# Sample rows and expert logits through column groups, gate/up weights in quarters, loops written out

## What is computed

```
proj    = rmsnorm(x) @ w_in                      # 53 column tiles of 128
mixers  = rwkv7, pooling, conformer conv, mamba2 SSD   # sequential, 128 rows a turn
merged  = sum_k (branch_k @ w_branch_k) * gate_k
x       = x + merged @ w_out                     # 1032 x 1024 x 1024
h       = rmsnorm(x)
logits  = h @ [w_group | w_expert]               # 4 + 16 = 20 columns
gate    = top-1 group, top-2 experts in it
x       = x + sum_e gate_e * (silu(h @ Wg_e) * (h @ Wu_e)) @ Wd_e   # 16 experts, hidden 256
y       = rmsnorm(x)
```

## Time and profile before

| what | us |
|---|---|
| three runs | 1785.87, 1785.58, 1779.35 (median 1785.58) |
| the profiled execution | 1770.31 |
| its span, first to last instruction | 1768.6 |

### The profile page before, as it was taken

One profiled execution on the slowest core, in us unless ns is written; L12 is line 12 of the kernel. 1 busy time (PEld: TensorE's weight loads), 2 busy tenths in 40 slices (PEclk: granted clock), 3 DMA queues, 4 the chain that ended last, 5 costly groups with the idle time before them and its releaser, 6 DMA issues.

```text
span 1768.6 us, 21208 instructions
## 1 busy us (share of the span) xinstructions
PE 1585.7 (90%) x7922; PEld 997.6 (56%) x7922; DVE 673.8 (38%) x1259; ACT 367.1 (21%) x648; POOL 189.4 (11%) x296
## 2 busy tenths in 40 slices
PE   8999799997799999999999999999999588978950
PEld 5666466564577777777777765666445432322310
DVE  5040079545434345343353432577112401101108
ACT  3110231130232313313133135100012111101102
POOL 3008100030101011010110000000000011101100
PEclk9999899998899999999999999999999689989985
DMA  6111101154111111111111121455201378666636
GB/s 191 36 36 36 28 25 36 36 92 47 59 35 48 45 47 46 39 42 44 48 45 43 38 98 44 153 229 208 81 24 60 119 285 340 241 242 226 218 128 264
DMA packets 38614, 181.38 MB, mean 103 GB/s; under 512 B 5448, under 2 KB 5864, under 8 KB 29440
## 3 DMA queue, kind: packets, MB, share of 16 engines
q1 hardware_dynamic: 22384, 114.03, 18.7%
q0 software_dynamic: 16144, 66.10, 11.4%
HBM read 336.93 MB, written 38.21 MB: 212 GB/s over the span
## 4 chain that ended last, share of the span: by engine, by line
PE 83%; DMA 7%; DVE 5%; issue 2%; ACT 2%; SPq 0%; POOL 0%; DVEq 0%; ACTq 0%; POOLq 0%
PE ps L457 35%; PE ps L810 7%; PE ps L867 7%; PE ps L779 6%; PE ps L881 3%; DMA arena<-in_w_gu 3%; PE ps L724 3%; PE ps L638 2%; PE ps L633 2%; DMA scr<-h_rows,idx 2%; PE ps L616 2%; PE ps L643 2%; PE ps L472 1%; PE ps L798 1%; DVE arena L1657 1%
## 5 line engine op out<-in xcount | busy, mean ns | idle before, releaser
L457 PE MATMUL ps<-arena,wring 128*128 128x344 f32 x2208 | 669.2, 453 | 0.0
L457 PEld LDWEIGHTS ps<-arena,wring 128*128 128x128 f32 x2208 | 406.5, 190 | 192.9 <-issue 5.2
L867 PE MATMUL ps<-arena,scr 128*32 128x512 f32 x1280 | 151.4, 625 | 22.9 <-DMA arena<-in_w_gu 22.9
L1739 POOL DMA_DIRECT2D gate_scratch<-stage x96 | 52.0, 542 | 759.1 <-ACT stage L1020 524.3
L810 PE MATMUL ps<-arena 128*128 128x512 f32 (+1 forms) x288 | 125.6, 594 | 1.2 <-DVE arena L1511 1.2
L779 PE MATMUL ps<-arena,wring 128*128 128x344 f32 x384 | 111.2, 451 | 0.0
L867 PEld LDWEIGHTS ps<-arena,scr 128*32 128x32 f32 x1280 | 41.4, 114 | 118.4 <-issue 98.0
L779 PEld LDWEIGHTS ps<-arena,wring 128*128 128x128 f32 x384 | 72.5, 189 | 38.6
L810 PEld LDWEIGHTS ps<-arena 128*128 128x128 f32 (+1 forms) x288 | 50.7, 178 | 71.0 <-issue 69.2
L881 PE MATMUL ps<-arena,scr 128*32 128x512 f32 x640 | 77.1, 625 | 13.3 <-issue 11.9
L1637 DVE TENSOR_TENSOR scr<-scr,ps 128x256 f32<-128x256 f32 x20 | 8.4, 422 | 190.0 <-ACT scr L1137 190.0
(11 more groups left out here) (397 smaller groups left out, 1848.8 us busy)
## 6 DMA issues: line engine op xcount, KB each, us to landing
arena<-in_w_gu SPq DMA_DIRECT2D x160, 1024.0 KB
arena<-in_w_dn SPq DMA_DIRECT2D x80, 1024.0 KB
wring<-in_w_all SPq DMA_DIRECT2D x61, 512.0 KB, 3.7
gate_scratch<-stage POOLq DMA_DIRECT2D x96, 172.0 KB, 2.2
arena<-gate_scratch POOLq DMA_DIRECT2D x4, 2064.0 KB, 8.5
scr<-gate_scratch POOLq DMA_DIRECT2D x4, 2064.0 KB, 9.0
arena<-y_rows SPq DMA_DIRECT2D x16, 512.0 KB, 9.5
arena<-in_w_out SPq DMA_DIRECT2D x2, 2048.0 KB, 11.2
```

What stands on the lines that cost most here:

```text
L457: mm = pe.matmul(ps[:, c, 0:CW], wring[:, slot, k, :], H[:, k, chunk(c)], start=k == 0, stop=k == KT - 1)
L867: mm = pe.matmul(ps[S * j:S * (j + 1), i % 2, :], XT[i % 2][:, k * P + S * j:k * P + S * (j + 1)], GU[j][:, k * 2 * HID:(k + 1) * 2 * HID] ...
L1739: pool.dma_start(gate_scratch[:, bass.ds(base + g, 1), chunk(c)], stage[:, c:c + 1, :]).then_inc(sem(f"gate_out{c}"), 16)
```

## The change

1. The ninth block of the output projection (8 sample rows) no longer has eight products of its own. `sample_parts` forms them in four column groups: the last 32 rows of `H` as a stationary side of 32 columns, each group with two of the eight k tiles, so four partial sums land in four groups of 32 partitions. ScalarE copies them (`sample_copy`), and one product with a constant (`pick8`) adds the four and picks the 8 rows. The block comes second in each half (`ORD`), no longer last.
2. The expert logits swap sides and use column groups as well: `w_r`, padded from 20 to 32 columns, is stationary, the turned rows are streamed (128 columns), ScalarE copies the partial sums (`logits_copy`), and one product with `pick20` (`logits_sum`) adds them and gives rows by 20 columns again. It comes one block later.
3. Gate/up weights are loaded and waited for in four quarters of k (`GUC = 4`), 512 KB each, with four pairs of semaphores.
4. All loops of all engines are written out; waits have constant values. One family of semaphores (`x_in`) is merged into another (`rows_in`).

```diff
+GUC = 4
             def load_gu(i, h):
-                w = GUW // 2
+                w = GUW // GUC
...
-            load_gu(0, 0)
-            load_gu(0, 1)
+            for h in range(GUC):
+                load_gu(0, h)
             load_dn(0)
...
             for i in range(STEPS - 1):
                 if i + 2 < STEPS:
                     look_up(i + 2)
-                    sp.wait_ge(sem("gu_mm0"), NS * (i + 2))
-                    load_gu(i + 2, 0)
-                    sp.wait_ge(sem("gu_mm1"), NS * (i + 2))
-                    load_gu(i + 2, 1)
+                    for h in range(GUC):
+                        sp.wait_ge(sem(f"gu_mm{h}"), NS * (i + 2))
+                        load_gu(i + 2, h)
...
-            with pe.Fori(0, NITER // 2) as i2:
+            for i2 in range(0, NITER // 2):
...
+            def logits(p):
+                m = rows_of(ORD[p])
+                pe.wait_ge(sem("hf_ev"), p + 1)
+                if p:
+                    pe.wait_ge(sem("lc_ev"), p)
+                for s in range(2):
+                    for g in range(4):
+                        mm = pe.matmul(ps[32 * g:32 * g + 32, 3, 256:256 + m], w_r[:, 2 * g + s, :],
+                                       HF[:, p % 2, 2 * g + s, 0:m], start=s == 0, stop=s == 1)
+                        if s == 1:
+                            mm.then_inc(sem("lg_mm"), 1)
+            def logits_sum(p):
+                n, m = ORD[p], rows_of(ORD[p])
+                pe.wait_ge(sem("lc_ev"), p + 1)
+                pe.matmul(ps[0:m, 3, 20 * n:20 * n + 20], LC[:, p % 2, 0:m], cc("pick20"), start=True, stop=True
+                          ).then_inc(sem("r_mm"), 1)
+            def sample_parts(h):
+                for s in range(2):
+                    for g in range(4):
+                        mm = pe.matmul(ps[32 * g:32 * g + 32, 4, :], H[:, 2 * g + s, T - 32:T], WO[h][:, 2 * g + s, :],
+                                       start=s == 0, stop=s == 1)
...
-                for n in range(NTT):
+                if h:
+                    pe.wait_ge(sem("smp_c"), 1)
+                sample_parts(h)
+                for p, n in enumerate(ORD):
...
+                    if m < P:
+                        pe.wait_ge(sem("smp_c"), h + 1)
+                        mm = pe.matmul(ps[0:m, q % 3, :], cc("pick8"), SMC, start=True, stop=True)
...
+                    if h == 1:
+                        if p >= 2:
+                            turn(p - 2)
+                        if p >= 4:
+                            logits_sum(p - 4)
+                        if p >= 3:
+                            logits(p - 3)
+            for p in range(NTT, NTT + 4):
+                if p - 2 < NTT:
+                    turn(p - 2)
+                logits_sum(p - 4)
+                if p - 3 < NTT:
+                    logits(p - 3)
...
             def gate_up(i):
...
-                    if k % 4 == 0:
-                        pe.wait_ge(sem(f"gu_in{k // 4}"), 16 * NS * (i + 1))
+                    if k % (KT // GUC) == 0:
+                        pe.wait_ge(sem(f"gu_in{k * GUC // KT}"), 16 * NS * (i + 1))
...
-                        if k % 4 == 3:
-                            mm.then_inc(sem(f"gu_mm{k // 4}"), 1)
+                        if (k + 1) % (KT // GUC) == 0:
+                            mm.then_inc(sem(f"gu_mm{k * GUC // KT}"), 1)
```

More of the change, by code:

```diff
@@ L120, in constants @@
     put("pick20", np.eye(32)[i % 32, 0:20])
+    put("pick8", np.eye(32)[i % 32, 32 - NSMP:])
+    put("pick20", np.eye(32)[i % 32, 0:20])
     put("dummy", 2 * T + 1 + i[:, None] + P * np.arange(STEPS)[None, :])
@@ L133, in __call__ @@
         self.n += 1
[L134 to L144, removed]
+        self.eng.wait_ge(self.sem, self.n)
 def build(nc, ins, outs):
@@ L295, in build @@
         HF = carve(0, 2, KT, P)
-        w_r = kk[:, 0, 0:KT * 20].rearrange("p (k m) -> p k m", k=KT)
+        SMC, LC = carve(8 * T, HALF), carve(8 * T + HALF, 2, P)
+        ORD = [0, NTT - 1] + list(range(1, NTT - 1))
+        w_r = kk[:, 0, 0:KT * 32].rearrange("p (k m) -> p k m", k=KT)
         RO = 3 * T
@@ L352, in _ @@
             load(1, 1)
-            with sp.Fori(1, N_BR0 // 2 + 1) as j:
+            for j in range(1, N_BR0 // 2 + 1):
                 sp.wait_ge(sem("dense"), 6 * j - 3)
@@ L461, in pairs @@
             def pairs(j0, j1):
-                with pe.Fori(j0, j1) as j:
+                for j in range(j0, j1):
                     for c in range(NCH):
@@ L926, in _ @@
             evac(S_R + 2, 6)
-            with act.Fori(1, 3) as j:
+            for j in range(1, 3):
                 evac(2 * j + S_R + 1, 6 * j + 3)
                 evac(2 * j + S_R + 2, 6 * j + 6)
-            with act.Fori(3, 6) as j:
+            for j in range(3, 6):
                 evac(2 * j - 6, 6 * j + 3)
@@ L948, in _ @@
                 inverse_root(LL[:, t, :], LL[:, t, :])
-            with act.Fori(6, 10) as j:
+            for j in range(6, 10):
                 evac(2 * j - 6, 6 * j + 3)
@@ L1060, in _ @@
             spread(0)
-            with act.Fori(0, NITER - 1) as i:
+            for i in range(0, NITER - 1):
                 turn(i, True)
@@ L1117, in _ @@
-            turned_out(NTT - 2)
-            turned_out(NTT - 1)
+            sample_copy(0)
+            sample_copy(1)
+            for p in range(NTT + 3):
+                if p < NTT:
+                    norm_row(p)
+                if 0 <= p - 2 < NTT:
+                    turned_out(p - 2)
+                if p >= 3:
+                    logits_copy(p - 3)
             act.wait_ge(sem("r_pre"), 1)
@@ L1375, in _ @@
             dve.wait_ge(sem("pre_done"), 2)
-            with dve.Fori(0, NITER) as i:
-                link.enter(i, PER_TURN)
+            for i in range(0, NITER):
                 nc.vector.tensor_copy(PCS, pc[:, :, bass.ds(2 * i, 2)])
@@ L1528, in _ @@
             for h in range(2):
-                for n in range(NTT):
-                    m, q = rows_of(n), NTT * h + n
+                for p, n in enumerate(ORD):
+                    m, q = rows_of(n), NTT * h + p
                     dve.wait_ge(sem("out_mm"), q + 1)
@@ L1654, in _ @@
                 for c in range(2):
[L1655 removed]
+                    dve.wait_ge(sem(f"rows_in{n}"), 32 + (16 if n < len(X_PARTS) else 0))
                     r_ = X2[0:m, n, :]
@@ L1778, in _ @@
             spread(0)
-            with pool.Fori(0, NITER - 1) as i:
+            for i in range(0, NITER - 1):
                 turn(i, True)
```

136 lines of the change are left out of this document (65 added, 71 removed).

## The result

| | median us | range | runs |
|---|---|---|---|
| before, beside the changed kernel | 1782.46 | 1777.62 to 1785.87 | 4 |
| changed | 1747.97 | 1739.45 to 1751.28 | 4 |
| before, later, beside it again | 1775.55 | 1771.06 to 1784.57 | 11 |
| changed, again | 1739.71 | 1738.21 to 1746.0 | 5 |

The ratio of changed to before is 0.9833 (95% interval 0.9801 to 0.9865) the first time and 0.9797 (0.9769 to 0.9825) the second: 30 to 36 us faster. The two intervals overlap, so either may be the nearer one. Forecast were 1748 us, and 37.5 us of gain.

A forecast was written before the change was run, and what follows sets the result against it. TensorE was taken to bound the kernel, with 83% of the chain of waits. Gains of 14 (sample rows, logits, end), 20 (quarters) and 3.5 (loops) make 37.5, off the median 1785.6: 1748 us, range 1732 to 1768.

The forecast's parts named there:

- Sample rows, logits, end: Output projection: sample rows and expert logits in column groups, plus the stage's end, 8.3 + 4.7 + 1 = 14 us gained (8 to 17).
- The toll for going between forms: Output projection: changing tiling mode drains TensorE, at most 0.2 us each; 0.3 taken off for two entries, all eleven 2 us.
- Quarters: Experts: gate/up loads issued 1.75 us earlier and less work behind the last landing, 20 us gained (5 to 32).
- The waits for gathers and down weights: Experts: 27.3 us of TensorE's waits, staying for the most part; an eighth, 3.5 us, gained (from 5 lost to 8 gained).
- heavy places: Four expert steps where two or three streams change expert at once, 4 to 6 MB; 18.3 us gained before gather losses.
- a gather: First heavy expert step: the gather issued at 1473.40 may land late, up to 3.4 us lost, 2 taken.
- They do two things: Experts: quarters issue the first load 1.75 us earlier and leave a quarter's products, not a half's, behind the last landing.
- the quarters add no bandwidth: Heavy expert steps: the DMA engines are already full, so smaller gate/up pieces move no more bytes.
- The rival that gathers and down weights take over: Experts: blocks ending sooner wait for the same bytes, so quarters give 3 us instead of 20: 1765 us; chance 0.20.
- The premise of the other: Experts: equal row sizes give gathers half of a full engine; quarters 32, all together 50, so 1736 us; chance 0.11.
- Loops: Turns: written-out loops shorten waits at loop edges and in VectorE's chain, 3.5 us gained (3 lost to 8 gained).
- SyncE: Rival, 20 expert steps: SyncE's issues become the bound from 0.55 us each; at 0.65, 13.6 us a step, 1806 us; chance 0.02.

The follow-up runs named there:

- quarters alone: The kernel before with gate/up weights loaded and waited for in four pieces and nothing else changed: 1759.25 us, ratio 0.9896 to before.
- the fine wait alone: The changed kernel with each quarter's loads issued only when its half of products is done, products still waiting for single quarters: 1757.27 us, ratio 0.9892 to before.
- the early issue alone: The changed kernel with TensorE waiting for two quarters at a time, loads still issued by quarters: 1754.03 us, ratio 0.9872 to before.
- the eighths: The changed kernel with gate/up weights in eight pieces a stream and one release counter for four semaphores: 1842.26 us, ratio 1.0371 to before.

## Why the prediction came out

**Sample rows, logits, end: 14 predicted, 14.7 and 15.1 in the two pairs of traces.** A group product was put at 0.219 us, eight at 1.75, measured 1.93; the pick product at 0.865, measured 0.95. The logits were put at 0.6, between bounds of 0.46 and 1.24; they are 0.57, near the bound that goes by the columns streamed. The sum was put at 0.21 and took 0.13. The count was off by one: before, logits stood in front of five blocks of the second half, not six, so the five gains that the sum used are all that were there. At the end, from the last block's products to the last logits, 10.2 us became 8.6 (1366.61 to 1375.20): 1.6 gained for the 1 taken.

The toll for going between forms is in the rows: a full block that follows products in column groups takes 7.06 us, and one that follows only the turning takes 6.87, as the one such block before did. That is 0.19 us, the size that the earlier trace rows had bounded at 0.2; seven blocks behind groups pay it, 1.3 us of this stage. Not all of it is new: before, the four full blocks behind the old logits, whose stationary side is 128 columns wide, took 6.96 us. Against them the toll is 0.10. The Trainium skill says that a change of mode drains the engine (TensorEngine Tiling (Array Packing), Key Properties) and gives no price. The trace agrees with it, at 0.10 to 0.19 us each, but doesn't single it out: the block behind `pick8` in the second half, a product with 8 stationary columns and no groups, took 7.06 us as well (1309.43 to 1316.49).

**Quarters: 20 predicted; 18.5 timed alone, 17.1 timed inside the change** (0.9893 less 0.9797, times 1777; 10.7 with the first comparison's 0.9833). The stretch ahead of the first gate/up product, in which the first gather lands, is 1.4 us shorter. The waits for gathers and down weights, of which the sum took 3.5 us off 27.3, fell by 2.5, to 24.8. The heavy places, as the time from one step's first gate/up product to the next, less 11.68, summed over the place:

| heavy place | before (two traces) | predicted gain | changed (two traces) | quarters alone |
|---|---|---|---|---|
| first, 1479 us | 10.0, 8.3 | 3.4 | 12.7, 9.1 | 9.3 |
| second, 1554 | 21.0, 21.0 | 4.8 | 18.9, 16.9 | 17.1 |
| third, 1617 | 9.4, 11.1 | 3.4 | 7.1, 5.9 | 2.8 |
| fourth, 1685 | 7.0, 7.0 | 4.7 | 3.1, 2.9 | 1.3 |

The first gained nothing or little. What was saved in waits for gate/up weights went to the others. TensorE's waits at that place, before (1472 to 1506) and in the changed kernel's second trace (1458 to 1492):

```profile
PE ps L867 <- DMA arena<-in_w_gu: 3.6, 2, 2.5
PE ps L881 <- issue: 2.2, 1, 2.2
PE ps L846 <- DMA scr<-h_rows,idx: 1.9, 1, 1.9
```

```profile
PE ps L874 <- DMA scr<-h_rows,idx: 3.1, 1, 3.1
PE ps L909 <- issue: 3.0, 2, 1.9
PE ps L895 <- DMA arena<-in_w_gu: 2.0, 2, 1.7
```

The prediction took 2 us off here for a gather, but for another one. It named the gather issued at 1473.40; its like in the changed kernel, issued at 1460.37, is not waited for. The one awaited is the next, issued at 1478.43. Before had waited for its like too (issued at 1492.52, 1.9 us), so 1.3 us are new and not 3.1. That this comes near the 2 taken is luck. A gather was awaited in before at the third place as well (1.7 us), where the prediction has them landing well ahead. From the second trace of the changed kernel:

```profile
1457.85 8.35 DMA arena<-in_w_gu
1466.24 1.92 PE ps L895 x16
1468.17 1.91 issue
...
1478.43 11.38 DMA scr<-h_rows,idx
...
1526.33 14.24 DMA arena<-in_w_gu
1540.62 1.92 PE ps L895 x16
...
1663.02 1.92 PE ps L895 x16
```

Behind a last landing stand 1.92 us of products (1.92 to 3.48 in the first trace), for the 5.34, 5.71 and 5.11 of the earlier trace rows; 1.75, 2.6 and 2.2 had been taken. So the numbers are near. The step that failed is "They do two things": an issue 1.75 us earlier and a shorter tail, as two gains that add. The runs put in its place one loop of load, product and release, in which the fine wait alone gave 0, the early issue alone 3.5 and the two 17.8. At the second heavy place the next step's loads start 5 us sooner behind the first's (12.5 for 17.4), not 1.75. Also wrong was "the quarters add no bandwidth": the engines were full inside the long wait that the earlier trace rows shows, but only 0.76 busy over the whole heavy place, with some 6 us of nothing right behind that wait. And the cold clock had been counted only in the tails, while it moves the products of the whole stage by 7 us from one execution to the next.

The rival that gathers and down weights take over (1765) holds for the first place alone. The premise of the other, that gathers get half of a full engine once the rows are of equal size, was right, by the two pairs of queue rows above. Its gain didn't come: 12.1 us of waits for gathers are left of 15.4, 9.3 of them the first.

**Loops: 3.5 predicted, 2.5 to 2.9 in the traces, 7.5 timed (4.8 to 10).** The wait at the start of turns fell from 6.9 to 4.7 us, 0.7 at most, and the three loop edges are gone.

**The sum.** 37.5 for 30 to 36: 1.5 to 3 too much for quarters by the second comparison (9 by the first), 1 too little for sample rows and logits, perhaps 4 too little for loops, and the rest within what the measurements leave open. That the predicted time fits to a tenth is luck: the median of before that it was taken from, 1785.58, was 3 us above the one measured beside the changed kernel.

**SyncE.** It was given little chance, rightly for quarters. By the rows of the eighths sixteen skipped loads are 7.3 us, with down loads (1.5) and the table (0.9) about 10 in place of the 9 predicted (an estimate), of the 11.68 that a step lasts; and it still waited 37 us for TensorE's gate/up products. The issues do show in the chain, 2% of the span where they were 0: among the experts (second trace) it now runs through 28 us of SyncE's loads and their table reads, 7 before. These cost little, as the DMA engines were already 0.86 busy in the first 2 us of such an issue (1516 to 1518 in the second trace). But 36 issues a step are past the limit, as the rival had it, through the number of issues more than their price: 0.46 us a skipped load, under the 0.55 from which it was to decide.

## What to carry to other kernels

Where a single buffer is loaded, used and loaded again piece by piece, cut issue, wait and release together; each alone may give nothing. Look at the DMA share over a whole heavy stretch, not inside its longest wait: at 0.76 there was room that the finer pieces used, in a dry spell behind each last landing, and at 0.94 further reordering gave nothing. Cutting pieces also changes who gets the engines: in the rows above both queues moved the same number of packets, so smaller rows on one mean fewer bytes for it. Count the issues of the queue before cutting finer: at 20 a step they were hidden, at 36 they cost 103 us. And take a second trace of both kernels before reading a gain out of a stage whose waits depend on transfers.

## What the runs showed of the hardware that was not expected

- A load that its condition skips costs SyncE 0.46 us (14.63 / 32) with its table reads; with eight of 32 running, the mean is 0.52 (16.79 / 32), or 0.27 more for each that runs. Skipping saves the bytes, hardly the issue.
- With equal gaps (30.9 and 31.4 us) two executions of one kernel had TensorE busy for 249.5 and 241.9 us over the same records, by the granted clock alone (0.94 and 0.97).
- Two DMA queues on full engines moved the same number of packets (225 and 227, 232 and 222), whatever the rows' sizes: 278 and 143 GB/s with rows of 8 and 4 KB, 210 each with 4 KB in both.
- Timed and traced gains of the written-out loops differ, 7.5 against 2.8 us; the traced pair is unequal by 5.6 us, and no run here tells where the rest lies.
